# Second block's heads: key stage first, and the query root as the scale of the softmax

## The reference

```python
def rms_norm(x, g):
    xf = x.astype(jnp.float32)
    y = xf * lax.rsqrt(jnp.mean(xf * xf, axis=-1, keepdims=True) + EPS)
    return (y * g.astype(jnp.float32)).astype(x.dtype)
...
    q = rms_norm(q.reshape(B, L, N_Q_HEADS, HEAD_DIM), q_g)
    k = rms_norm(k.reshape(B, L, N_KV_HEADS, HEAD_DIM), k_g)
...
        q_l = apply_axial_rope(q_l, cos, sin)
        k_l = apply_axial_rope(k_l, cos, sin)
        k_all = jnp.concatenate([k_c, k_l], axis=1)
        v_all = jnp.concatenate([v_c, v_l], axis=1)
        o_l = latent_attention(q_l, k_all, v_all)
...
    s = jnp.einsum('btkgd,blkd->bkgtl', q, k, preferred_element_type=jnp.float32) * (HEAD_DIM ** -0.5)
    p = jax.nn.softmax(s, axis=-1).astype(v.dtype)
```

## Time and profile before

| | |
|---|---|
| median of 3 runs | 2943.74 us (2941.03 to 2947.94) |
| span of the profiled execution | 2941.1 us |
| TensorE busy | 2757.6 us, 94% |
| VectorE busy | 1478.2 us, 50% |
| ScalarE busy | 791.4 us, 27% |
| mean granted TensorE clock | 0.956 |

### The profile page before, as it was taken

The page is one execution under the profiler, slowest core; times in us unless marked ns, Lnnn a source line. Parts: engine busy times, 40 slices in busy tenths (PEclk is TensorE's granted clock), DMA queues, the critical chain, the costliest instruction groups (busy, mean ns, idle before and its releaser), DMA issues.

```text
span 2941.1 us, 34419 instructions
## 1 busy us (share of the span) xinstructions
PE 2757.6 (94%) x12400; PEld 2152.2 (73%) x12400; DVE 1478.2 (50%) x2513; ACT 791.4 (27%) x1048; POOL 322.4 (11%) x243
## 2 busy tenths in 40 slices
PE   7999999888898999989999999999987799999998
PEld 5888877544457888858888888788874556788886
DVE  6777785556648755573222222444235553433334
ACT  3212122235533212142211111222321352331222
POOL 0101110000002111111202202103000002110111
PEclk9999999868699999999999999999998899999999
DMA  4544442200033544422122221133321001223321
GB/s 132 149 129 145 130 125 71 52 15 1 1 111 97 150 136 143 132 75 57 59 70 57 68 61 47 54 100 100 90 89 44 15 1 59 84 86 100 100 82 61
DMA packets 394758, 241.03 MB, mean 82 GB/s; under 512 B 14768, under 2 KB 392752, under 8 KB 394672
## 3 DMA queue, kind: packets, MB, share of 16 engines
q1 hardware_dynamic: 394672, 239.92, 27.9%
HBM read 237.79 MB, written 2.10 MB: 82 GB/s over the span
## 4 chain that ended last, share of the span: by engine, by line
PE 84%; DVE 9%; ACT 4%; issue 1%; POOL 1%; DMA 1%; SPq 0%; DVEq 0%; ACTq 0%; POOLq 0%
PE PS L564 21%; PE PS L567 21%; PE PS L565 21%; PE PS L550 3%; PE PS L551 3%; PE PS L553 3%; PE PS L528 2%; PE PS L906 2%; PE PS L680 1%; DVE SA L1485 1%; DVE VA L1175 1%; PE PS L886 1%; DVE RB L1159 1%; PE PS L773 1%; POOL VA L1592 1%
## 5 line engine op out<-in xcount | busy, mean ns | idle before, releaser
L564 PE MATMUL PS<-NH,WH 128*128 128x512 f32 x2160 | 814.5, 377 | 25.8 <-DVE NL L1165 11.5
L565 PE MATMUL PS<-NL,WH 128*128 128x512 f32 x2160 | 792.0, 374 | 0.0
L567 PE MATMUL PS<-NH,WL 128*128 128x512 f32 x2160 | 751.1, 374 | 0.0
L1154 DVE TENSOR_TENSOR WL<-RAW,WH 128x2048 fp32r<-128x2048 f32 x190 | 462.0, 2431 | 111.2 <-ACT WH L933 109.9
L933 ACT ACTIVATE WH<-RAW 128x2048 fp32r<-128x2048 f32 x190 | 363.8, 1915 | 572.4 <-PE PS L567 533.1
L564 PEld LDWEIGHTS PS<-NH,WH 128*128 128x128 f32 x2160 | 408.0, 189 | 120.5 <-issue 27.9
L565 PEld LDWEIGHTS PS<-NL,WH 128*128 128x128 f32 x2160 | 408.2, 189 | 70.1
L567 PEld LDWEIGHTS PS<-NH,WL 128*128 128x128 f32 x2160 | 384.3, 190 | 58.1
L564 PE MATMUL PS<-HH,WH 128*128 128x512 f32 x880 | 329.4, 374 | 1.2 <-DVE WL L1154 1.2
L1194 DVE SCALAR_TENSOR_TENSOR RB<-MW,CV,RB 128x128 f32<-128x128 f32 x826 | 319.5, 419 | 17.8
L565 PE MATMUL PS<-HL,WH 128*128 128x512 f32 x880 | 320.1, 373 | 0.0
(11 more groups left out here) (222 smaller groups left out, 2639.5 us busy)
## 6 DMA issues: line engine op xcount, KB each, us to landing
RAW<-in_ffn_w_in SPq DMA_DIRECT2D x88, 512.0 KB, 4.7
MW<-in_w_mod SPq DMA_DIRECT2D x72, 512.0 KB, 3.8
RAW<-in_w_in SPq DMA_DIRECT2D x70, 512.0 KB, 4.3
RAW<-in_w_gate SPq DMA_DIRECT2D x44, 512.0 KB, 4.1
RAW<-in_w_up SPq DMA_DIRECT2D x44, 512.0 KB, 5.3
RAW<-in_w_down SPq DMA_DIRECT2D x32, 512.0 KB, 4.4
RAW<-in_ffn_w_out SPq DMA_DIRECT2D x32, 512.0 KB, 3.9
RAW<-in_w_out SPq DMA_DIRECT2D x16, 512.0 KB, 4.4
```

The lines of the kernel that those rows point to most:

```text
L564: pe.matmul(o, wh, xh(k), start=k == 0, stop=False)
L565: pe.matmul(o, wh, xl(k), start=False, stop=False)
L567: last = pe.matmul(o, wl, xh(k), start=False, stop=k == kn - 1)
L1154: dve.tensor_tensor(WL[1 - s][:, :], RAW[1 - s][:, :], WH[1 - s][:, :].bitcast(F32), ALU.subtract).then_inc(w_lo, 1)
```

## The change

The key stage comes first and the query stages after it. The context's key products go to bank 5, no longer to the query stages' banks.

For keys, square, sum and root stay as they were in form, but the gain alone is applied ahead of swap and rotation (`L1522` and `L1525` of the changed kernel), and the inverse root, kept in the memory of `PT2` as `KR`, is multiplied into the rotated keys during the value stage. Sums and swaps of the keys stand in the first query stage, behind its first half; the three roots behind them on ScalarE; the three reciprocals one each in the three later query stages.

For queries, the gain alone is applied too. The sum over features is now made per 128 tokens as a product of the squares (as weights) with one column of ones: four products of one column a head, all into one bank, 32 columns in all. Sums and swaps of one stage stand behind the first half of the next stage, those of the last behind the second value tile. One root and one reciprocal of 128x32 elements (`RQ`), times 1/sqrt(128), end the value stage. Each unit of attention uses a column of `RQ` as the scale of the exponential and as the factor of the maximum, where the constant stood.

```diff
-        q_b, k_b, v2_b = plan(HC // 2), plan(1), plan(1)
+        k_b, q_b, v2_b = plan(1), plan(HC // 2), plan(1)
...
-            b, other, half, tok = HN[i][:4]
-            return (G, U)[half][(b + other) % 2][:, 0:tok]
+        KR = PT2[:, :, :, :].rearrange("p s e q -> p (s e q)")
+        KXB = [(G, U)[h][k_b % 2] for h in range(KVC)]
+        KCB = [B[5][:, h * TC:(h + 1) * TC] for h in range(KVC)]
+        def q_bank(i):
+            return (G, U)[i % 2][(q_b + i // 2) % 2]
+        def v2_bank(t):
+            s = v2_b % 2
+            return B[(2 * s, 2 * s + 1, 2 - 2 * s, 3 - 2 * s)[t % 4]][:, 0:2 * P]
+        def q_root(g, e, q):
+            return RQ[:, (g * 4 + e) * NT + q:(g * 4 + e) * NT + q + 1]
...
+            pairs(k_b, 1, w_in2, 0, KD, 4096, True)
             pairs(q_b, HC // 2, w_in2, 0, KD, 3072)
-            pairs(k_b, 1, w_in2, 0, KD, 4096, True)
             pairs(v2_b, 1, w_in2, 0, KD, 4352, True)
             pairs(ba_b, KD // 2, inp["w_branch_attn_2"][0], 0, KD, 0)
             pairs(wo2_b, KD // 2, inp["w_out_2"][0], 0, KD, 0)
...
-            def head_sums(b):
-                for i in hn_of(b):
-                    tok = HN[i][3]
+            def key_sums():
+                for i in range(2 * KVC):
+                    pe.wait_ge(hk_sq, i + 1)
+                    if i == KVC:
+                        pe.wait_ge(hk_z, 2 * KVC)
+                    h = i % KVC
+                    o = B[6 + h] if i < KVC else KCB[h]
+                    at = slice(0, T) if i < KVC else slice(T, T + TC)
+                    pe.matmul(o, ones[:, :], SA[:, h, at], start=True, stop=True).then_inc(hk_mm, 1)
+            def key_swaps():
+                pe.wait_ge(hk_sq, KVC)
+                for h in range(KVC):
+                    pe.wait_ge(hk_z, h + 1)
+                    pe.matmul(KXB[h], PX[:, :], VA[:, h, 0:T], start=True, stop=True).then_inc(hk_sw, 1)
+            def head_sums(n):
+                for i in (2 * n, 2 * n + 1):
                     pe.wait_ge(hn_sq, i + 1)
+                    for t in range(NT):
+                        last = pe.matmul(B[4][:, i * NT + t:i * NT + t + 1], SA[:, i % 2, t * P:(t + 1) * P],
+                                         ones[:, 0:1], start=True, stop=True)
+                    last.then_inc(hn_mm, 1)
+            def head_swaps(n):
+                for i in (2 * n, 2 * n + 1):
+                    pe.wait_ge(hn_z, i + 1)
                     if i >= 2:
...
+                        pe.wait_ge(hn_out, i - 1)
+                    else:
+                        pe.wait_ge(hk_rms, 3)
+                    pe.matmul(B[6 + i % 2], PX[:, :], VA[:, i % 2, 0:T], start=True, stop=True).then_inc(hn_sw, 1)
             pe.wait_ge(b_loaded, 32)
             for n in range(HC // 2 + 1):
-                b = q_b + n
+                b = k_b + n
                 s = b % 2
...
+                begin(b)
                 for half in range(2):
                     def wt(k):
                         c = (k * 2 + half) * P
                         return WH[s][:, c:c + P], WL[s][:, c:c + P]
                     if b == k_b:
-                        last = tile([(G, U)[half][s][:, :], (G, U)[half][1 - s][:, 0:TC]], wt, XCS, KD,
-                                    (norm_lo, norm_c2.low))
+                        last = tile([KXB[half], KCB[half]], wt, XCS, KD, (norm_lo, norm_c2.low))
                     else:
...
+                        last = tile([(G, U)[half][s]], wt, XS, KD)
+                        if half == 0 and b == q_b:
+                            key_sums()
+                            key_swaps()
+                        elif half == 0:
+                            head_sums(n - 2)
+                            head_swaps(n - 2)
                 last.then_inc(pe_done, 1)
...
+            begin(v2_b)
             s = v2_b % 2
             for t in range(TK // P):
+                if t == 2:
+                    head_sums(HC // 2 - 1)
+                    head_swaps(HC // 2 - 1)
+                    pe.wait_ge(psum_free, v2_b)
                 if t >= 4:
                     pe.wait_ge(v2_out, t - 3)
                 c = (T + t * P) % TK
                 for k in range(KD):
                     xh, xl = (z[:, k, c:c + P] for z in (NH, NL))
                     wh, wl = (z[s][:, k * 2 * P:(k + 1) * 2 * P] for z in (WH, WL))
-                    o = B[t % 4][:, 0:2 * P]
+                    o = v2_bank(t)
                     pe.matmul(o, xh, wh, start=k == 0, stop=False)
...
                 g, q, e = UNITS2[u]
+                if u == 0:
+                    pe.wait_ge(hk_out, KVC)
+                if q == 0 and e == 0:
+                    pe.wait_ge(hn_out, 4 * g + 4)
...
                     last = act.activation(o, (G, U)[half][s][:, :], ACT.Sigmoid)
                 last.then_inc(ga_done, 1)
-            for b in range(q_b, k_b + 1):
+            split(k_b % 2, loaded(k_b, 1), k_b)
+            act.wait_ge(pe_done, k_b + 1)
+            for h in range(KVC):
+                act.activation(SA[:, h, 0:T], KXB[h], ACT.Square).then_inc(hk_sq, 1)
+            for h in range(KVC):
+                act.activation(SA[:, h, T:T + TC], KCB[h], ACT.Square).then_inc(hk_sq, 1)
+            for b in range(q_b, v2_b):
                 split(b % 2, loaded(b, 1), b)
+                if b == q_b:
+                    for i, n in enumerate((1, 2, 4)):
+                        act.wait_ge(hk_mm, n)
+                        act.activation(KR[:, i * T:(i + 1) * T], B[(6, 7, 5)[i]], ACT.Sqrt, bias=eps[:, :],
+                                       scale=1.0 / P).then_inc(hk_rms, 1)
                 act.wait_ge(pe_done, b + 1)
...
+                for i in (2 * (b - q_b), 2 * (b - q_b) + 1):
+                    if i >= 2:
+                        act.wait_ge(hn_mm, i - 1)
+                    act.activation(SA[:, i % 2, 0:T], q_bank(i), ACT.Square).then_inc(hn_sq, 1)
             split(v2_b % 2, loaded(v2_b, 1), v2_b)
+            act.wait_ge(hn_mm, HC)
+            act.activation(RQ[:, :], B[4][:, 0:HC * NT], ACT.Sqrt, bias=eps[:, :], scale=1.0 / P).then_inc(hn_rms, 1)
             def exp2(u):
                 act.wait_ge(at2_m, u + 1)
                 if u >= 4:
                     act.wait_ge(at2_t, 2 * (u - 3))
+                g, q, e = UNITS2[u]
                 act.activation(p_slot2(u), PS[:, (u % 2) * 1024:(u % 2) * 1024 + TK], ACT.Exp,
-                               bias=stat(NM, u), scale=float(P) ** -0.5, accum_out=stat(DEN, u)).then_inc(at2_e, 1)
+                               bias=stat(NM, u), scale=q_root(g, e, q), accum_out=stat(DEN, u)).then_inc(at2_e, 1)
             def turned2(u):
                 n = u // 4
...
                 dve.sem_inc(psum_free, 1)
             dve.wait_ge(b_loaded, 32)
-            for b in range(q_b, k_b + 1):
+            def turned_by(dst, h, swapped, ready, n):
+                own.settle(dve, dve.tensor_tensor(RB[:, :], VA[:, h, 0:T], TX[:, 0, :], ALU.mult))
+                dve.wait_ge(ready, n)
+                own.settle(dve, dve.tensor_tensor(dst, swapped, TX[:, 1, :], ALU.mult))
+                own.settle(dve, dve.tensor_tensor(dst, dst, RB[:, :], ALU.add))
+            def q_turned(i):
+                turned_by(QT[:, i, :], i % 2, B[6 + i % 2], hn_sw, i + 1)
+                dve.sem_inc(hn_out, 1)
+            def key_inverse(i):
+                dve.wait_ge(hk_rms, i + 1)
+                own.settle(dve, dve.reciprocal(KR[:, i * T:(i + 1) * T], KR[:, i * T:(i + 1) * T]))
+            split(k_b % 2, k_b)
+            for h in range(KVC):
+                dve.wait_ge(hk_sq, h + 1)
+                dve.tensor_scalar(VA[:, h, 0:T], KXB[h], vec("k_norm"), None, ALU.mult).then_inc(hk_z, 1)
+            dve.wait_ge(hk_sq, 2 * KVC)
+            for h in range(KVC):
+                dve.tensor_scalar(KT[:, h, 0:TC], KCB[h], vec("k_norm"), None, ALU.mult).then_inc(hk_z, 1)
+            dve.wait_ge(hk_z, 2 * KVC)
+            for b in range(q_b, v2_b):
+                n = b - q_b
                 split(b % 2, b)
...
+                if n == 0:
+                    for h in range(KVC):
+                        turned_by(KT[:, h, TC:TK], h, KXB[h], hk_sw, h + 1)
+                    dve.sem_inc(psum_free, 1)
+                else:
+                    q_turned(2 * n - 2)
+                    q_turned(2 * n - 1)
+                    key_inverse(n - 1)
+                for i in (2 * n, 2 * n + 1):
+                    dve.wait_ge(hn_sq, i + 1)
+                    dve.tensor_scalar(VA[:, i % 2, 0:T], q_bank(i), vec("q_norm"), None, ALU.mult).then_inc(hn_z, 1)
+                dve.wait_ge(hn_z, 2 * n + 2)
+                dve.sem_inc(psum_free, 1)
             split(v2_b % 2, v2_b)
             for t in range(TK // P):
                 dve.wait_ge(v2_mm, t + 1)
-                dve.tensor_copy(V2[:, t, :], B[t % 4][:, 0:2 * P]).then_inc(v2_out, 1)
+                dve.tensor_copy(V2[:, t, :], v2_bank(t)).then_inc(v2_out, 1)
```

(23 more changed lines are left out.)

60 lines of the change are left out of this document (removed).

## The result

| | before | after |
|---|---|---|
| median, taken in turn on one chip | 2942.39 us (2940.93 to 2947.94) | 2887.86 us (2885.38 to 2890.12) |
| span of the profiled execution | 2941.1 us | 2887.4 us (its own time 2889.41) |
| TensorE / VectorE / ScalarE busy | 2757.6 / 1478.2 / 791.4 us | 2744.3 / 1455.1 / 787.6 us |
| mean granted clock | 0.956 | 0.964 |

The ratio is 0.9813, with a 95% interval of 0.9801 to 0.9826: 54.5 us faster. The forecast was 2885.

The account below looks back on a forecast made before the run. Bound: VectorE's queue order and head normalisation's latency. Stages 16.7 + 15.2 + 42.4 + 21.1 = 95.4 us replace 155.8, 60.4 less; waits 0.5 and pointers 1.1 leave 58.8 off 2943.7: 2885 us, range 2879 to 2897.

Parts of the forecast that it names:

- The bound: Query and key stages: VectorE's queue order and head normalisation's latency bound the 155.8 us stretch, not any engine's throughput.
- Key stage: Key stage, now first: 48 products of 512 columns and 48 of 256, 16.7 us, with no wait for earlier heads.
- First query stage: First query stage: its own products, 10.9 us, plus the key sums and swaps, 4.3 us, make 15.2 us.
- its cover: First query stage: half its products, 5.45 us, hide the 4 us of key squares and gains, 1.5 us to spare.
- Query stages two to four: Later three query stages: products 10.9, eight one-column sums 1.5, two swaps 1.7; 14.1 us each, 42.4 us for three.
- Value stage to first score: Value stage: products 17.3 us, last sums and swaps 3.2, copy ahead of the first score 0.6; 21.1 us.
- Pointers: Attention: exponential and tiny product ahead of it read their scale from a column; 1.1 us more, between nothing and 5.0.
- VectorE's slack: Query stages two to four: reciprocal ends 1 us into the next stage, gains needed 6.9 us in; some 4 us in hand.
- the first (2895): Attention pointers fully exposed and one-column sums at separate loads: 4 + 6 us on top, 2895 us; chance 0.09.
- The second (2897): Query stages: VectorE becomes the bound, a stage takes 17 us; 9 us more, value stage 3 more, 2897 us; chance 0.06.
- the fourth (2914): Stretch's work hidden less than it looks, half the gain going into an unseen wait: 2914 us; chance 0.04.
- The third: Key stage to value stage's end: TensorE stays at 1.2 GHz, 35 us slower than before, 2980 us; chance 0.02.

Follow-up runs that it names:

- The three kernels that start from before: Kernel before with the next weights' split ahead of the head work, 2923.95 us; with the heads' reciprocals left out, 2912.93 us; with both edits, 2900.35 us.
- the constant scale: Changed kernel with constant 1/sqrt(128) again as the exponential's scale and the maximum's factor, query root left out of the result: 2880.28 us, 0.9794 of the kernel before.

## Why the prediction was right, step by step

- **The bound** was named rightly: queue order and exposed latency, not throughput. The three kernels that start from before show both, and leave 19.5 us to the tails as the third part.
- **Key stage**: 16.7 against 16.85 us measured. **First query stage**: 15.2 against 15.25, and its cover held: no idle of TensorE ahead of the key sums or swaps.
- **Query stages two to four**: 14.1 against 14.43 each. The one-column sums were sized from two of them beside a large product at 1.5 us for eight and take 1.71; the rest, 0.1 us, lies around the swaps and was not traced. Over three stages that is 1.0 us, inside the bound that I gave.
- **Value stage to first score**: 21.1 against 21.7; 0.2 is the sums, 0.15 the wait for the last copy (0.76 against 0.61); the rest I did not trace.
- The sum 95.4 and 0.5 for waits, 95.9, stand against 97.08, so the stretch is 58.7 us shorter where 59.9 were forecast. TensorE's idle inside it is 0.76 us, once, ahead of the first score.
- **Pointers**: 1.1 us against 0.7 measured, by the traces and by the constant scale. ScalarE's idle ahead of its copies gave its part back: in consecutive units 0.34 and 0.19 us became 0.25 us and none. The section "What ACT_TABLE_LOAD costs" of "ScalarE: Activation LUTs" in the Trainium skill says that each pointer adds about 93 ns; the runs agree for the second one (995 against 904 ns). The 3.0 us that the prediction worked out from that figure for 32 units, an estimate for the case that nothing hides it, did not show.
- **Total**: 58.8 forecast, 58.0 between the two profiles once the unchanged part is taken out. The two errors, 1.2 us too little for the stages and 0.4 us too much for the pointers, have opposite signs, which is a little luck. The medians of three sets of runs give 54.5, 58.2 and 61.0 us. The forecast of 2885 started from a median of 2943.7, the runs beside the result have 2942.4; that the measured median still lies 3 us above it is within what the unchanged parts move between executions.
- **VectorE's slack** was put at 4 us. The reciprocal ends at 2220.32, 1.2 us into the next stage (forecast: 1 us), the gains behind it end at 2221.77, and their swap is 7.16 us into the stage, at 2226.3: 4.5 us in hand. The two reciprocals put back, 6.7 us, used it up and made the stages 3 to 5 us longer.
- Of the rivals, the first (2895) wanted 3.0 us for a group of one-column sums and 5.0 for the pointers; they take 1.71 and 0.7. The second (2897) and the fourth (2914) would have shown an idle note or a stage of 17 us and more, and no query stage has either. The third, a clock at 1.2 GHz through the stretch, shows in no row of it.

## What to carry to other kernels

When a stage waits for an operand that another engine prepares, look first at what is queued ahead of that operand there, and move it ahead of work whose consumer comes later; then look for products that stand alone at a change of stages. Price the three (order, work, exposed tails) apart, since none of them was over half of this gain (16.9 and 24.9 us by runs, 19.5 as what was left, of 58.7). A row factor in front of a softmax is cheap as its scale: 0.7 us for 32 units here, in place of eight reciprocals of 3.35 us.

## What the runs showed of the hardware

- **A short wait can cost more than its length.** Idle of 0.69 us ahead of the one-column sums made a stage of 14.4 us into one of 17.1, with a granted clock of 0.55 to 0.60 for 4 us behind it, in two query stages of three (and a mean of 0.93 in the value stage), the same in both executions; 3.38 us of idle cost 5.3. The same sums without the idle ahead of them, in the changed kernel, left the clock at 1.00, and so did a longer idle without them: in the kernel with the split first, 1.78 us ahead of the second swap left it at 1.00 in two whole stages (16.4 us each). In these runs so short an idle went with a fall only next to the one-column sums; why is not shown.
- **The clock of unchanged parts differs by execution.** Attention takes 121.8 us at a mean clock of 1.00 and 124.7 at 0.97, with the same instructions; the start of the stretch moves by 11 us over the thirteen profiles. Terms of 1 us are read from the stretch, not from the span.
- **One-column products** take 1.71 us for eight, 0.107 us a record (each product is two records), as long as two products of 512 columns of the same kind.
- **A second pointer** costs the exponential 91 ns, and one costs the 128x1 product on VectorE 60 ns (154 to 214).
- **ScalarE's copy of 32 rows** by 512 to other partitions takes 629 ns; four replace a product of two records that holds TensorE for some 0.86 us (half of the 1.7 us by which a stage became shorter).
